# Summing compressed attention probabilities on GpSimd, with one transposed tile per head pair

## The reference, cut to what matters

```python
def nsa_cmp_attend(q, t, kc, vc):
    end = jnp.arange(nc) * CMP_STRIDE + CMP_LEN - 1
    s = jnp.einsum('bqkgd,bckd->bkgqc', q, kc) * SCALE
    p = masked_softmax(s, end[None, :] <= t[:, None])
    o = jnp.einsum('bkgqc,bckd->bqkgd', p.astype(vc.dtype), vc)
...
    return gb[:, :, 0] * o_c + gb[:, :, 1] * o_s + gb[:, :, 2] * o_w
...
    o = gates[:, :, 0] * o_c + gates[:, :, 1] * o_s + gates[:, :, 2] * o_w
```

## Time and profile before

| | us |
|---|---|
| median of 3 runs | 939.9 (939.66 to 943.08) |
| the profiled execution, whole | 939.63 |
| its span, first to last instruction | 937.8 |
| TensorE busy | 895.2 |
| TensorE loading weights (beside it) | 811.5 |
| VectorE busy | 524.2 |
| ScalarE busy | 413.7 |
| GpSimd busy | 291.0 |

### The profile page before, as it was taken

How to read it: one execution, slowest core, us unless ns; L and a number is a source line. 1 busy time by engine, 2 the same in 40 slices (tenths; PEclk the granted TensorE clock), 3 DMA queues, 4 the chain that set the end, 5 groups by cost and what they waited for, 6 DMA issues and landing times.

```text
span 937.8 us, 20464 instructions
## 1 busy us (share of the span) xinstructions
PE 895.2 (95%) x7594; PEld 811.5 (87%) x7594; DVE 524.2 (56%) x1501; ACT 413.7 (44%) x1063; POOL 291.0 (31%) x495
## 2 busy tenths in 40 slices
PE   6899999999999999999999999899999999999997
PEld 6899999999999899999988787768877787778885
DVE  4557332322323665645666787676777858844443
ACT  6434221224443011113466676565775667832221
POOL 0223212222223635435135153324422526410000
PEclk9999999999999999999999999999999999999999
DMA  7564414324240443231849058714604142343331
GB/s 230 156 206 136 151 45 152 103 88 121 67 145 25 132 142 98 95 105 63 219 132 284 4 160 264 255 57 119 181 2 131 56 141 77 102 137 133 128 121 67
DMA packets 85220, 117.91 MB, mean 126 GB/s; under 512 B 12930, under 2 KB 67506, under 8 KB 84546
## 3 DMA queue, kind: packets, MB, share of 16 engines
q1 hardware_dynamic: 71666, 73.12, 27.4%
q0 software_dynamic: 10224, 36.20, 11.5%
q10 hardware_dynamic: 3232, 7.28, 2.2%
HBM read 91.50 MB, written 32.02 MB: 132 GB/s over the span
## 4 chain that ended last, share of the span: by engine, by line
PE 78%; DVE 6%; issue 6%; ACT 5%; DMA 2%; POOL 2%; ACTq 0%; DVEq 0%; SPq 0%; POOLq 0%
PE psum L601 8%; PE psum L1866 7%; PE psum L602 7%; PE psum L603 7%; PE psum L1745 6%; PE psum L1722 4%; PE psum L1887 3%; PE psum L1886 3%; PE psum L1885 3%; PE psum L1723 3%; ACT p_P L1975 2%; PE psum L842 2%; PE psum L844 2%; PE psum L843 2%; PE psum L825 2%
## 5 line engine op out<-in xcount | busy, mean ns | idle before, releaser
L601 PE MATMUL psum<-a_whi,f_xhi 128*128 128x256 f32 (+1 forms) x672 | 194.7, 290 | 4.2 <-DVE a_hst L1127 2.6
L602 PE MATMUL psum<-a_wlo,f_xhi 128*128 128x256 f32 (+1 forms) x672 | 190.0, 283 | 0.0
L603 PE MATMUL psum<-a_whi,f_xlo 128*128 128x256 f32 (+1 forms) x672 | 189.6, 282 | 0.0
L1975 ACT ACTIVATE p_P<-psum,p_nb 128x640 f32<-128x640 f32 (+7 forms) x224 | 124.2, 561 | 45.8 <-DVE p_nb L2047 37.7
L601 PEld LDWEIGHTS psum<-a_whi,f_xhi 128*128 128x128 f32 x672 | 127.1, 189 | 6.9 <-DVE a_hst L1127 2.8
L602 PEld LDWEIGHTS psum<-a_wlo,f_xhi 128*128 128x128 f32 x672 | 127.2, 189 | 0.0
L603 PEld LDWEIGHTS psum<-a_whi,f_xlo 128*128 128x128 f32 x672 | 127.2, 189 | 0.0
L744 POOL DMA_DIRECT2D h_scratch<-a_hst x93 | 50.8, 548 | 211.7 <-DVE a_hst L1127 103.1
L1745 PE MATMUL psum<-f_ident,p_P 128*128 128x128 f32 x656 | 99.3, 275 | 1.4 <-ACT s_KTw L1925 0.7
L1745 PEld LDWEIGHTS psum<-f_ident,p_P 128*128 128x128 f32 x656 | 76.8, 140 | 8.0 <-DVE p_PT L1913 2.1
L2047 DVE CUSTOM_DVE_ANT_0 psum<-psum,p_near 128x256 f32<-128x256 f32 (+7 forms) x96 | 64.6, 673 | 31.2 <-PE psum L1723 25.3
(11 more groups left out here) (340 smaller groups left out, 2168.0 us busy)
## 6 DMA issues: line engine op xcount, KB each, us to landing
a_wraw<-in_w_in SPq DMA_DIRECT2D x24, 512.0 KB, 4.4
h_scratch<-a_hst POOLq DMA_DIRECT2D x72, 128.0 KB, 3.4
s_SG<-in_cache_nsa_slc SPq DMA_DIRECT2D x64, 128.0 KB, 2.3
p_qd<-q_scratch SPq DMA_DIRECT2D x16, 384.0 KB, 7.5
a_xraw<-in_x_prompt SPq DMA_DIRECT2D x8, 512.0 KB, 7.0
s_MK<-in_cache_mem SPq DMA_DIRECT2D x8, 512.0 KB, 8.6
s_WG<-in_cache_nsa_win SPq DMA_DIRECT2D x8, 512.0 KB, 5.3
mix_scratch<-p_zt POOLq DMA_DIRECT2D x8, 512.0 KB, 3.5
```

Of the source, the lines that this page charges most:

```text
L601: nc.tensor.matmul(out, hi, wh, start=first, stop=False)
L602: nc.tensor.matmul(out, hi, wl, start=False, stop=False)
L603: return nc.tensor.matmul(out, lo, wh, start=False, stop=last)
L1975: nc.scalar.activation(dst, s_view(s), ACT.Exp, bias=nb[:, g % NNB:g % NNB + 1], scale=1.0 if s[2] == 3 else -1.0, accum_out=ssum[:, par[i ...
```

## The change

- The exponentials of the compressed branch of a pair of heads go into one tile `PCM` of 128x128 (two buffers), head g in columns 0 to 63 and head g + 4 in 64 to 127, without `accum_out`.
- Only the second unit of a pair (l%4 = 3) has the compressed tile to transpose, and it serves both heads. The values' tile `VC[:, 8]` becomes block diagonal (key/value head 0 in rows 0 to 63, head 1 in rows 64 to 127, zeros elsewhere), so that each head's product takes its own half of the transposed rows. The products keep their number. A pair whose second unit has one chunk more than its first gets a product step of that chunk alone. This happens for tile 3, whose first units have 4 tiles and whose second have 5.
- The sums over 64 columns come from a tree of six additions on GpSimd, at the place of the second unit's `sm` in the list of steps, each waiting for the one before. VectorE's weights of a block wait for the sums (`p_cs`), and an exponential into a `PCM` buffer waits for the sum two pairs back.
- The sample's mix runs as five steps in five successive groups of the schedule: three gate products (two with an addition), two z products, and the last product with the store. The wait for the gathered results is in the first.
- `gf` moves to the place of `KM` in memory, and its load behind the last score product, ahead of the first load of x. The zero fill of `P` and its waits go; a small zero fill of `VC` comes in at the kernel's start.

```diff
@@ setup
+    csm = ru("csm", [128, 2, 32])
+    PCMs = [ru(f"PCM{i}", [128, 128]) for i in range(2)]
-    gf = rd("gf", [128, D])
+    gf = nc.alloc_sbuf_tensor_at("d_gf", [128, D], F32, offset=km_at)
+    cmp_pair = {}
+    for v, (_, l) in enumerate(UNITS):
+        if l < 16 and l % 4 >= 2:
+            cmp_pair[v] = len(cmp_pair) // 2
@@ tiles_of
-        return [(a, k, 128) for a, s in enumerate(softmaxes(v)) for k in range((s[5] + 127) // 128)]
+        sms = softmaxes(v)
+        if sms[-1][2] == 2:
+            return [(0, k, 128) for k in range(sms[0][5] // 128)] + [(1, 0, 128)] * (UNITS[v][1] % 2)
+        return [(a, k, 128) for a, s in enumerate(sms) for k in range(s[5] // 128)]
@@ sample_groups
-        groups += [[("load_fin", 0)], [], [("fin", 0)], [], [], [], []]
+        groups += [[("load_fin", 0)], [], [("fin", 0)], [("fin", 1)], [("fin", 2)], [("fin", 3)], [("fin", 4)]]
@@ schedule
-                    waiting.append((partner[len(mine) - 1], mine[-1]))
+                    waiting.append((partner[len(mine) - 1] if len(mine) <= len(partner) else mine[-1], mine[-1]))
@@ sp_attend, load_m and load_x
                     sp.wait_ge(S("s_mxo"), 16)
-                    sp.dma_start(gf[:], io["ln_final"].rearrange("(o n) -> o n", o=1).to_broadcast([128, D])).then_inc(S("d_const"), 16)
...
                     sp.wait_ge(S("p_qk"), NV)
+                    sp.dma_start(gf[:], io["ln_final"].rearrange("(o n) -> o n", o=1).to_broadcast([128, D])).then_inc(S("d_const"), 16)
@@ transposes
-                if v in (2, 3):
-                    pe.wait_ge(S("p_zero"), 2)
...
-                    l = nc.tensor.transpose(o[0:w, 128 * j:128 * j + 128], P[v % 2][:, at:at + w], ident[:])
+                    probs = PCMs[cmp_pair[v] % 2][:] if sms[a][2] == 2 else P[v % 2][:, at:at + w]
+                    l = nc.tensor.transpose(o[0:w, 128 * j:128 * j + 128], probs, ident[:])
@@ act_attend
+                    if s[2] == 2:
+                        k = cmp_pair[v]
+                        if k >= 2:
+                            act.wait_ge(S("p_cs"), k - 1)
+                        nc.scalar.activation(PCMs[k % 2][:, s[7]:s[7] + NC], s_view(s), ACT.Exp, bias=nb[:, g % NNB:g % NNB + 1], scale=-1.0).then_inc(S("p_exp"), 1)
+                        continue
@@ weights
             dve.wait_ge(S("p_exp"), sm_count(last_of_block[n]))
+            dve.wait_ge(S("p_cs"), 1 + max(k for v, k in cmp_pair.items() if v <= last_of_block[n]))
@@ pool_mix_sample(pool, ch, n)
+        if n == 0:
+            pool.wait_ge(S("on_in"), 16 * 2 * NDB)
+            pool.wait_ge(S("s_z"), 64)
+        if n < 3:
+            ch.step(pool.tensor_tensor(on_s[:, :, n], on_s[:, :, n], g[:, :, n].to_broadcast([NS_TOK, 8, HD]), ALU.mult))
+            if n:
+                ch.step(pool.tensor_tensor(on_s[:, :, 0], on_s[:, :, 0], on_s[:, :, n], ALU.add))
+        elif n == 3:
+            pool.tensor_tensor(zs[:, 512:768], OC[0:NS_TOK, QT], zs[:, 512:768], ALU.mult).then_inc(S("s_mix"), 1)
+            pool.tensor_tensor(zm, om_s[:], zm, ALU.mult).then_inc(S("s_mix"), 1)
+        else:
+            pool.tensor_tensor(z, on_s[:, :, 0], z, ALU.mult).then_inc(S("s_mix"), 1)
+            pool.wait_ge(S("s_mix"), 3)
+            pool.dma_start(mD[T:T + NS_TOK, :], zs[:]).then_inc(S("s_mxo"), 16)
@@ pool_attend
-        for i in range(2):
-            pool.memset(P[i][:, 704:768], 0.0).then_inc(S("p_zero"), 1)
...
+            elif what == "sm" and UNITS[n][1] < 16 and UNITS[n][1] % 4 == 3:
+                s, k = softmaxes(n)[1], cmp_pair[n]
+                pool.wait_ge(S("p_exp"), sm_count(n))
+                both = PCMs[k % 2][:].rearrange("p (j c) -> p j c", j=2)
+                ch.step(pool.tensor_tensor(csm[:], both[:, :, 0:32], both[:, :, 32:64], ALU.add))
+                for h in (16, 8, 4, 2):
+                    ch.step(pool.tensor_tensor(csm[:, :, 0:h], csm[:, :, 0:h], csm[:, :, h:2 * h], ALU.add))
+                pool.tensor_tensor(ssum[:, par[UNITS[n][0]], s[1] - 1:s[1] + 1].rearrange("p (j o) -> p j o", o=1), csm[:, :, 0:1], csm[:, :, 1:2], ALU.add).then_inc(S("p_cs"), 1)
```

More of the change, by code:

```diff
@@ L297, in build @@
     V = rp("V", [128, 2, QT, 128])
+    km_at = rp.at
     KM = rp("KM", [128, 4, NM], F32R)
@@ L704, in pool_trunk @@
         pool.memset(VC[64:128], 0.0).then_inc(S("vc_zero"), 1)
-        pool.wait_ge(S("vc_zero"), 1)
+        pool.memset(VC[0:64, NDB, HD:128], 0.0).then_inc(S("vc_zero"), 1)
+        pool.wait_ge(S("vc_zero"), 2)
         pool.wait_ge(S("x_tr"), 6)
@@ L860, in second @@
                     for b in range(nb):
-                        o = 512 * 7 + 128 * b + 64 * kv
-                        i = nc.tensor.matmul(psum[0:64, o:o + 64], h[:, nb * kv + b], w2[:, 1], start=True, stop=True)
+                        o, r = 512 * 7 + 128 * b + 64 * kv, 64 * kv if u == NDB // 2 else 0
+                        i = nc.tensor.matmul(psum[r:r + 64, o:o + 64], h[:, nb * kv + b], w2[:, 1], start=True, stop=True)
             i.then_inc(S("c_l2"), 1)
@@ L1077, in keep @@
             elif v == 1:
-                i = nc.vector.tensor_copy(VC[0:64, NDB, :], psum[0:64, 512 * 7:512 * 7 + 128])
+                dve.wait_ge(S("vc_zero"), 2)
+                nc.vector.tensor_copy(VC[0:64, NDB, 0:HD], psum[0:64, 512 * 7:512 * 7 + HD])
+                i = nc.vector.tensor_copy(VC[64:128, NDB, HD:128], psum[64:128, 512 * 7 + HD:512 * 7 + 128])
             else:
@@ L1372, in softmaxes @@
             c_at = base + 512 + (n // 2 if i == QT - 1 else 448)
-        return [(at, 6 * g + 2 + j, 1, h, k0, n, halves, 0), (at + 1, 6 * g + 4 + j, 2, h, 0, 64, [(c_at, NC)], 640)]
+        return [(at, 6 * g + 2 + j, 1, h, k0, n, halves, 0), (at + 1, 6 * g + 4 + j, 2, h, 0, 64, [(c_at, NC)], 64 * j)]
     def score_parts(v):
@@ L1703, in pe_attend @@
         assert last % 4 == 0 and all(by_act(j) for j, _ in proj_jobs[last - 3:])
-        pe.wait_ge(S("vc_zero"), 1)
+        pe.wait_ge(S("vc_zero"), 2)
         pe.wait_ge(S("p_kw"), 2)
@@ L1842, in pv @@
         def pv(pair):
-            v = p_chunks[pair[0]][1]
+            v = p_chunks[pair[1]][1]
             i, l = UNITS[v]
@@ L1850, in pv @@
             if l >= 16:
-                sides = [[(p, k, 128) for p, (a, k, _) in enumerate(p_chunks[pair[0]][2]) if a == j] for j in range(2)]
+                sides = [[(pair[0], p, a, k) for p, (a, k, _) in enumerate(p_chunks[pair[0]][2]) if a == j] for j in range(2)]
             else:
-                sides = [[(p, k, w) for p, (_, k, w) in enumerate(p_chunks[pair[0]][2])]] * 2
+                own = [[(c, p, a, k) for p, (a, k, _) in enumerate(p_chunks[c][2]) if a == 0] for c in pair]
+                both = [(pair[1], p, a, k) for p, (a, k, _) in enumerate(p_chunks[pair[1]][2]) if a == 1]
+                sides = [own[j] + both for j in range(2)]
             for m in range(len(sides[0])):
                 for j in range(2):
-                    p, k, w = sides[j][m]
-                    vj = v if l >= 16 else v + j
-                    a = j if l >= 16 else p_chunks[pair[j]][2][p][0]
+                    c, p, a, k = sides[j][m]
+                    vj = v if l >= 16 else v - 1 + j
                     _, num, b, h, k0, keys = softmaxes(vj)[a][0:6]
@@ L1864, in pv @@
                     kv = HD * (h // 4)
-                    val = VM[:, k, HD * h:HD * h + HD] if b == 3 else VC[0:w, NDB, kv:kv + HD] if b == 2 else V[:, b, k0 + k, kv:kv + HD]
-                    i_mm = nc.tensor.matmul(psum[64 * j:64 * j + 64, at:at + 128], val, PTs[p_rank[pair[j]] % NPT][0:w, 128 * p:128 * p + 128],
+                    val = VM[:, k, HD * h:HD * h + HD] if b == 3 else VC[:, NDB, kv:kv + HD] if b == 2 else V[:, b, k0 + k, kv:kv + HD]
+                    i_mm = nc.tensor.matmul(psum[64 * j:64 * j + 64, at:at + 128], val, PTs[p_rank[c] % NPT][0:128, 128 * p:128 * p + 128],
                                             start=k == 0, stop=128 * (k + 1) >= keys, skip_group_check=True)
@@ L1966, in act_attend @@
                     wait_norm(act, last_block[prev[i]])
-                if v < 2 and i > 4:
-                    act.wait_ge(S("p_zero"), 2)
                 act.wait_ge(S("p_nb"), sm_count(v))
@@ L2204, in dve_attend, with pool_mix_sample @@
                 dve.wait_ge(S("d_y"), 2 * n + 2)
-    def pool_mix_sample(pool, ch):
+    def pool_mix_sample(pool, ch, n):
         z = zs[:, 0:512].rearrange("p (h d) -> p h d", d=HD)
         zm = zs[:, 768:1024].rearrange("p (h d) -> p h d", d=HD)
-        ch.do(pool.tensor_tensor(zs[:, 512:768], OC[0:NS_TOK, QT], zs[:, 512:768], ALU.mult))
-        ch.do(pool.tensor_tensor(zm, om_s[:], zm, ALU.mult))
-        ch.step(pool.tensor_tensor(on_s[:, :, 0], on_s[:, :, 0], on_s[:, :, 1], ALU.add))
-        ch.step(pool.tensor_tensor(on_s[:, :, 0], on_s[:, :, 0], on_s[:, :, 2], ALU.add))
-        pool.tensor_tensor(z, on_s[:, :, 0], z, ALU.mult).then_inc(S("s_mix"), 1)
+        g = gs[:].rearrange("p (r h o) -> p h r o", r=3, o=1)
```

(10 more changed lines are left out.)

## The result

The changed kernel takes 949.3 us (median of 4 runs, 949.0 to 950.8), the kernel before 939.8 beside it (939.6 to 943.1): ratio 1.0103, 95% interval 1.0078 to 1.0127. It is slower by 1.0%. The forecast was 945.6 with a range to 949.5: the sign and the three places were right, the size was 3.7 us short. The profiled execution has a span of 949.0 us inside 950.8, against 937.8 inside 939.6.

A forecast was written before the change was run, and what follows sets the result against it. TensorE was taken to bound the attention stage, with GpSimd's queue order deciding the change: 939.6 - 2.9 - 1.1 - 0.3 + 1.9 + 0.8 + 7.3 = 945.3, 945.6 us by the median, range 936.5 to 949.5.

The forecast's parts named there:

- Transposes, accumulators and copies: Attention stage: fewer transposes save 2.9 us, exponentials without accumulators 1.1, narrower copies 0.3.
- Unit 8: Start of attention: the first GpSimd sum stands ahead of tile 1's query split, which TensorE awaits; +1.9 us.
- Block 12: Unit 47's sum stands between GpSimd's load_z wait and the gates VectorE's weights need; +0.8 us.
- Block 33: Unit 123's sum stands behind the sample mix's DMA wait and steps, so TensorE waits; +7.3 us, bounds 5.5 to 9.
- the 8 us named in advance: Sign in the profile: VectorE idle about 8 us at a reciprocal near 785 us, released by GpSimd's last addition.
- gf and the mix in steps: The final gain's later load costs nothing, up to 1 us if transfers crowd; the stepped mix has no separate term.
- The sum: Step adding all terms to the profile's 939.6 us: 945.3, or 945.6 by the median.
- (a): The forecast itself: all three GpSimd sum waits cost time; 945.6 us, own range 942 to 948, chance 0.55.
- (d): Rival: GpSimd additions take 0.46 us or VectorE shuts them out, many blocks late; 949 to 951 us, chance 0.15.
- (b): Rival: the wait at block 33 is hidden; 938.3 us, chance 0.2.
- (c): Rival: shorter exponentials close TensorE's waits for them in the attention stage; 931 to 934 us, chance 0.10.

The follow-up runs named there:

- e3: Changed kernel with compressed row sums through ScalarE's accumulator and no sums on GpSimd; 937.1 us, ratio 0.9967.
- e8: Changed kernel with row sums through ScalarE's accumulator, while GpSimd still makes all 32 trees, read by nobody; 943.1 us, ratio 1.0049.
- e11: As e8, without the trees of units 3 and 47, the other 30 still unread; 939.4 us, ratio 0.9999.
- after: The changed kernel itself, against the kernel before; 949.3 us, ratio 1.0103.
- e1: Changed kernel with the five sample mix steps at units 125 to 129 instead of 118 to 122; 948.1 us, ratio 1.0095.
- e2: Changed kernel with all five sample mix steps at unit 118, ahead of the sum of unit 123; 954.9 us, ratio 1.017.
- e5: Changed kernel with the five sample mix steps at units 121 to 125, right behind the sum of unit 123; 945.5 us, ratio 1.007.
- e6: Changed kernel with each pair's sums made by one reduction on VectorE, none on GpSimd; 936.7 us, ratio 0.9969.
- e7: Changed kernel with mix step 0 and its DMA wait at unit 118, steps 1 and 2 at 121, 3 and 4 at 122; 950.6 us, ratio 1.0125.
- e9: Changed kernel, GpSimd reordered: first sum behind two parts of tile 1's query split, mix steps at units 121, 122 and 125; 943.5 us, ratio 1.0039.
- e10: Changed kernel with only the first pair's sum moved behind the first two parts of tile 1's query split; 952.1 us, ratio 1.0128.
- e12: Changed kernel with e9's mix placement, first sum ahead of the query split, GpSimd's eight sample memsets behind its first two parts; 938.3 us, ratio 0.9992.
- e4: Kernel before with only the sample mix in five steps and gf's new place and load; 939.9 us, ratio 1.0001.

## Why the prediction was right in sign and short in size

The prediction's own sum was 945.3, for an execution that took 950.8. The lag table gives each term.

- **Transposes, accumulators and copies: -4.3 foreseen, -3.0 measured** (won: 0.6 to unit 6, 1.0 from 10 to 50, 0.3 from 54 to 68, 1.4 from 70 to 126; lost: 0.3 from 132 to 142). From unit 10 to 50, nine pairs, the kernels that keep the reads (e3, e8, e11) gain 0.6 us and those without them (after, e1, e2, e5, e6, e7, e9, e10, e12) 1.0; from 70 to 126, twelve pairs, e3 gains 0.8 and those without reads 1.4 to 1.6. So a saved transpose with its narrower copy is worth 0.06 to 0.07, not 0.11: this was oversized, and why isn't shown. A pair's two reads are worth 0.04 to 0.06, 1.3 to 1.9 us for 32 pairs against 1.1 foreseen: that size was about right. Some 0.9 us are lost at unit 134 in every kernel with the pair tile, e3 and e6 too, and none in e4; this is in tile 3, where the forecast left -1 to +1.5 us for copies that change hands, and its cause stays open.
- **Unit 8: +1.9 foreseen, +4.1 measured.** The stop is 2.60 instead of 0.22 us, so the sum's 1.78 and the 0.6 that TensorE had won until then (the forecast had left pairs ahead of a stop out of its gain for this reason; counted its way it is -2.4 above and +3.5 here); then TensorE's clock is 0.66 in the stretch behind, 1.6 us. That term was missing. In e2 the same stop, 2.49 us, had no fall of the clock behind it, and only 2.4 us were lost.
- **Block 12: +0.8 foreseen, +1.0 measured.** Right.
- **Block 33: +7.3 foreseen, +9.5 measured.** The mechanism, the queue's order and the size of the stop (7.62 us) were as written; VectorE's idle time (7.71) was the 8 us named in advance. The sum came at 793.7, not 792.8: the wait ended 1.8 us later than before, and what stood between it and the sum took 7.5 us instead of 8.3. What this term left out is again the clock, 0.50 from 795 to 800 us: 1.9 us beyond the stop.
- **gf and the mix in steps: nothing foreseen, nothing measured** (e4: 1.0001).
- **Outside the sum:** a fall of the clock at 640 us, +1.3 us, also in e3, e6 and e7; an earlier trunk, -1.6; and -0.1 in the tail. With them 945.3 + 1.3 + 2.2 + 0.2 + 2.2 + 1.3 - 1.6 - 0.1 = 950.8.

The step that failed is in "The sum": it priced each stop of TensorE at its length, and put a fall of the clock behind it at nothing, without a reason. The runs showed 1.6 us of slow clock behind unit 8 and 1.9 behind block 33; together with 1.3 us too much for transposes, accumulators and copies that is most of what was missing. 949.3 lies outside the 942 to 948 that the forecast gave to its own mechanism (a), and 0.2 us inside the whole range, which reached so far only to take in half of (d). That the range held is luck in this part.

Rival (b) is out, as TensorE stops in full. (c) is out too: in e6, with no accumulator reads and no wait for a sum on GpSimd, TensorE still waits 6.5 us in all for exponentials (6.7 before), and the time is 936.7, not 931 to 934. (d) is out as stated: 30 of the 32 trees took 1.77 to 1.81 us and two took 2.73, and no reciprocal but three stands waiting. Its number, 949 to 951, was met by another way.

## What to carry to other kernels

When work moves to an idle engine whose queue is in order, list for each new instruction what stands ahead of it that can wait (a DMA above all), and what stands behind it that somebody needs: here 57 us of trees were nearly all hidden, time was lost at three places, and some 11 us of it came back at two of them by moving what nobody waits for. A step that is moved has a deadline as well as a start: the mix had three (sum of 123, sum of 127, a weight split), and each placement that looked at fewer kept a stop of 4.4 us or more. And if the engine that already produces the values can sum them (e3), or another takes 0.28 us for it (e6), no queue needs mending.
